# The head norm of the recurrent branch, moved into the merge stage of a two-model decoder kernel

## What is computed

```python
y_ret = retention(q, k, v, g, positions, ret_gn_g)
y_rwkv = rwkv7_time_mix(p_rwkv, ...)     # recurrent branch, 8 heads of 64
y_conv = short_conv(p_conv, conv_w)
gates = jax.nn.sigmoid((h @ w_gate + b_gate).astype(F32))
merged = jnp.zeros(x.shape, F32)
for i, y in enumerate((y_ret, y_rwkv, y_conv)):
    merged = merged + gates[..., i * d:(i + 1) * d] * (y @ w_branch[i])
x = x + (gate1[:, None, :] * (merged.astype(x.dtype) @ w_o)).astype(x.dtype)
```

```python
mu = jnp.mean(yf, axis=-1, keepdims=True)
var = jnp.mean(jnp.square(yf - mu), axis=-1, keepdims=True)
y = (yf - mu) * lax.rsqrt(var + eps) * g
y = y + jnp.sum(r * kt * r_k.astype(F32), axis=-1, keepdims=True) * v
return (y.reshape(bsz, seq, mw) * g).astype(p.dtype)
```

## Time and profile before

| | |
|---|---|
| median of 3 runs | 2585.14 us (2583.62 to 2586.28) |
| the profiled execution: time | 2586.32 us |
| the profiled execution: span from first to last instruction | 2584.5 us |
| its mean granted TensorE clock | 0.909 |
| recurrent head norm, first layer | 1064.47 to 1075.16 us |
| merge, first layer | 1075.45 to 1202.94 us |
| recurrent head norm, second layer | 1938.12 to 1948.65 us |
| merge, second layer | 1948.95 to 2076.66 us |

### The profile page before, as it was taken

How to read it: one execution, slowest core, us unless ns; L and a number is a source line. 1 busy time by engine, 2 the same in 40 slices (tenths; PEclk the granted TensorE clock), 3 DMA queues, 4 the chain that set the end, 5 groups by cost and what they waited for, 6 DMA issues and landing times. The chain is left out here.

```text
span 2584.5 us, 33377 instructions
## 1 busy us (share of the span) xinstructions
PE 2083.0 (81%) x14160; PEld 1300.0 (50%) x14161; DVE 634.1 (25%) x1404; ACT 359.0 (14%) x725; POOL 76.8 (3%) x104
## 2 busy tenths in 40 slices
PE   7888778889777999899867666689989988666665
PEld 5564336564333688788522222238887873222222
DVE  4451003551002235454200000022441121000001
ACT  1520001520002021200100000011211020000000
POOL 0201000201000000000000000000000000000000
PEclk9999989999988999999897888899999989888887
DMA  9358999255999332286899999973312369999996
GB/s 385 132 230 363 429 429 401 116 228 218 429 428 399 114 130 99 112 340 273 340 428 428 428 428 428 429 302 130 131 36 98 131 246 395 428 429 428 429 429 286
DMA packets 55841, 779.34 MB, mean 302 GB/s; under 512 B 6840, under 2 KB 7096, under 8 KB 8120
## 3 DMA queue, kind: packets, MB, share of 16 engines
q1 hardware_dynamic: 55736, 777.82, 72.5%
HBM read 776.75 MB, written 1.05 MB: 301 GB/s over the span
## 5 line engine op out<-in xcount | busy, mean ns | idle before, releaser
L1925 PE MATMUL bank<-ring,xnT 128*32 128x512 f32 x3136 | 488.6, 761 | 307.5 <-DMA ring<-in_w_exp 303.7
L1925 PEld LDWEIGHTS bank<-ring,xnT 128*32 128x32 f32 x3136 | 102.0, 125 | 683.7 <-DMA ring<-in_w_exp 450.3
L1950 PE MATMUL bank<-ring,arena 128*32 128x512 f32 x1440 | 178.6, 635 | 65.2 <-DMA ring<-in_w_exp 45.3
L965 PE MATMUL bank<-xnT,ring 128*128 128x256 f32 x960 | 210.7, 379 | 0.0
L2113 DVE TENSOR_TENSOR arena<-bank,arena 128x256 f32<-128x256 f32 (+1 forms) x33 | 18.3, 554 | 748.3 <-PE bank L1925 528.1
L965 PEld LDWEIGHTS bank<-xnT,ring 128*128 128x128 f32 x960 | 181.6, 190 | 28.4 <-issue 4.5
L1631 PE MATMUL bank<-xnT,ring 128*128 128x256 f32 x768 | 176.9, 384 | 10.1 <-PEq L843 10.1
L1631 PEld LDWEIGHTS bank<-xnT,ring 128*128 128x128 f32 x768 | 148.1, 193 | 32.3 <-issue 11.7
L1888 PE MATMUL bank<-arena,xnT 128*128 128x256 f32 x592 | 145.0, 400 | 3.6 <-DVE xnT L2124 3.6
L1888 PEld LDWEIGHTS bank<-arena,xnT 128*128 128x128 f32 x592 | 115.0, 200 | 64.3 <-issue 49.0
L1880 PE MATMUL bank<-arena 128*128 128x128 f32 x1056 | 133.3, 288 | 3.4 <-DVE arena L2033 3.4
(11 more groups left out here) (425 smaller groups left out, 2046.1 us busy)
## 6 DMA issues: line engine op xcount, KB each, us to landing
ring<-in_w_exp SPq DMA_DIRECT2D x274, 2048.0 KB, 25.6
arena<-in_w_ada SPq DMA_DIRECT2D x24, 2048.0 KB, 12.1
ring<-in_w_in SPq DMA_DIRECT2D x20, 2048.0 KB, 26.0
ring<-in_w_merge SPq DMA_DIRECT2D x18, 2048.0 KB, 8.0
arena<-in_w_exp SPq DMA_DIRECT2D x14, 2048.0 KB, 14.2
ring<-in_w_o SPq DMA_DIRECT2D x8, 2048.0 KB, 10.4
ring<-in_w_conv SPq DMA_DIRECT2D x6, 2048.0 KB, 7.9
ring<-in_w_rest SPq DMA_DIRECT2D x2, 1696.0 KB, 25.8
```

Source lines behind the costliest of these rows:

```text
L965: last = nc.tensor.matmul(o[:, T * j:T * j + T], w[:, k, col:col + P], xnT[:, k, :], start=k == 0, stop=k == KT - 1)
L1925: last = nc.tensor.matmul(o[rows(e), :], Xw[:, k, rows(e)], w[:, at:at + MW], start=k == 0, stop=k == KT - 1)
L1950: last = nc.tensor.matmul(o[rows(e), :], hidT[:, j, rows(e)], w[:, at:at + MW], start=j == 0, stop=j == ft - 1)
```

## The change

The block `head_norm` is gone. Its instructions now stand inside `merge`, which takes the branches in the order retention, convolution, recurrent. The weight chunks, the gate bias and the list `ys` follow that order.

```diff
+        BRANCHES = (0, 2, 1)
...
-                load(sp, n, dram["w_merge2"][l, n - MERGE])
+                load(sp, n, dram["w_merge2"][l, 3 * BRANCHES[(n - MERGE) // 3] + (n - MERGE) % 3])
...
+            mean_made, flat, sq_ready, var_made, log_ready, rstd_ready, normed = (sem(f"nwkv_{x}") for x in ("mean", "flat", "sq", "var", "log", "rstd", "done"))
+            ys = [(y_ret, y_rwkv, y_conv)[b] for b in BRANCHES]
+            y, nsq, gain = y_rwkv, ar(13824, MT, T), V2("rwkv_gn_g_2")
...
-            sg = ar(13824, 4, T)
+            sg = ar(16896, 4, T)
...
                 @block.sync
                 def _(sp):
                     if ahead:
+                        sp.wait_ge(normed, 1)
                         sp.dma_start(c_raw, dram["c_row"]).then_inc(c_in, 16)
...
                 @block.tensor
                 def _(pe):
+                    for i in range(2):
+                        nc.tensor.matmul(bank[4 + i][:, :], K("blk64"), y[:, 2 * i:2 * i + 2, :], start=True, stop=True).then_inc(mean_made, 1)
                     for i in range(3):
                         n = MERGE + 3 * i
                         for d in range(KT):
                             m = KT * i + d
+                            if m == 1:
+                                for a in range(2):
+                                    pe.wait_ge(sq_ready, a + 1)
+                                    nc.tensor.matmul(bank[6 + a][:, :], K("blk64"), nsq[:, 2 * a:2 * a + 2, :], start=True, stop=True).then_inc(var_made, 1)
+                            if m in (4, 5):
+                                pe.wait_ge(flat, m - 3)
+                            if m in (6, 7):
+                                pe.wait_ge(log_ready, m - 5)
+                            if m == 2 * KT:
+                                pe.wait_ge(normed, 1)
...
                 @block.scalar
                 def _(act):
+                    nc.scalar.preload_act_table_set("natural_log_exp_and_others")
+                    for i in range(2):
+                        act.wait_ge(flat, i + 1)
+                        nc.scalar.activation(nsq[:, 2 * i:2 * i + 2, :], y[:, 2 * i:2 * i + 2, :], ACT.Square).then_inc(sq_ready, 1)
+                    for i in range(2):
+                        act.wait_ge(var_made, i + 1)
+                        nc.scalar.activation(nsq[:, 2 * i:2 * i + 2, :], pair_of(bank[6 + i]), ACT.Ln, scale=1.0 / HD, bias=REPS).then_inc(log_ready, 1)
+                        act.wait_ge(log_ready, i + 1)
+                        nc.scalar.activation(nsq[:, 2 * i:2 * i + 2, :], nsq[:, 2 * i:2 * i + 2, :], ACT.Exp, scale=-0.5).then_inc(rstd_ready, 1)
...
                 @block.vector
                 def _(dve):
                     then = step(dve, s_dve)
+                    for i in range(2):
+                        dve.wait_ge(mean_made, i + 1)
+                        nc.vector.scalar_tensor_tensor(y[:, 2 * i:2 * i + 2, :], pair_of(bank[4 + i]), -1.0 / HD, y[:, 2 * i:2 * i + 2, :], ALU.mult, ALU.add).then_inc(flat, 1)
+                    for j in range(MT):
+                        dve.wait_ge(rstd_ready, j // 2 + 1)
+                        last = nc.vector.scalar_tensor_tensor(y[:, j, :], y[:, j, :], gain[:, j:j + 1], nsq[:, j, :], ALU.mult, ALU.mult)
+                    then(last)
+                    then(nc.vector.tensor_tensor(y, y, bonus, ALU.add))
+                    nc.vector.tensor_tensor(y, y, gT, ALU.mult).then_inc(normed, 1)
...
-                head_norm("nwkv", y_rwkv, ar(13824, MT, T), "blk64", HD, REPS, V2("rwkv_gn_g_2"), rwkv_finish)
                 merge(l)
```

More of the change, by code:

```diff
@@ L834, in load2 @@
                 load(sp, n, dram["w_exp2"][l, n - MOE2])
[L839 to L875, removed]
@@ L1599, in merge, with pair_of @@
             pair_ready, gate_ready, taken, s_dve = sem("mrg_pair"), sem("mrg_gate"), sem("mrg_taken"), sem("mrg_dve")
-            ys = (y_ret, y_rwkv, y_conv)
+            mean_made, flat, sq_ready, var_made, log_ready, rstd_ready, normed = (sem(f"nwkv_{x}") for x in ("mean", "flat", "sq", "var", "log", "rstd", "done"))
+            ys = [(y_ret, y_rwkv, y_conv)[b] for b in BRANCHES]
+            y, nsq, gain = y_rwkv, ar(13824, MT, T), V2("rwkv_gn_g_2")
+            def pair_of(b):
+                return b[:, :].rearrange("p (a t) -> p a t", a=2)
             ada, c_in, c_ready = ada_sems(), sem("mrg_c"), sem("mrg_cready")
@@ L1654, in _ @@
                                 act.wait_ge(taken, m - 3)
-                            nc.scalar.activation(sg[:, m % 4, :], bank[m % 8][:, 0:T], ACT.Sigmoid, bias=V2("b_gate_2")[:, m:m + 1]).then_inc(gate_ready, 1)
+                            nc.scalar.activation(sg[:, m % 4, :], bank[m % 8][:, 0:T], ACT.Sigmoid, bias=V2("b_gate_2")[:, KT * BRANCHES[i] + d:KT * BRANCHES[i] + d + 1]).then_inc(gate_ready, 1)
                 @block.vector
@@ L1713, in _ @@
                     norm_rstd(dve, norms)
-        def rwkv_finish(then):
-            then(nc.vector.tensor_tensor(y_rwkv, y_rwkv, bonus, ALU.add))
-            nc.vector.tensor_tensor(y_rwkv, y_rwkv, gT, ALU.mult)
         WIN = 32
```

## The result

The changed kernel takes 2568.35 us (median of 13 runs, 2562.72 to 2575.35) against 2585.14 us for the one before (13 runs, 2575.58 to 2592.68). The ratio is 0.994 with an interval of 0.9928 to 0.9952: 15.5 us less, 12.4 to 18.6. The ratio is formed from all runs; the two medians by themselves differ by 16.8 us. The forecast was 2570.4 us in a range of 2566.8 to 2574.8, a gain of 14.7. A stretch repeats to 0.1 or 0.2 us where the clock falls at the same place.

A forecast was written before the change was run, and what follows sets the result against it. The norm was taken as bound by engines passing data in turn, TensorE idling 5.03 us before the merge. Gains of 7.36 + 7.37 = 14.7 us off 2585.14 gave 2570.4 us, range 2566.8 to 2574.8.

The forecast's parts named there:

- The stretch: First mean matmul to tile 1's first matmul: from 17.75 us per layer to 10.39 and 10.38, gaining 14.7 in all.
- The means: Start of the stretch: left slow, 3.18 and 3.02 us to the next matmul; at full clock a layer needs 8.64.
- The clock at tile 0: Tile 0's gate matmuls: no second clock fall without the idle time; 3.75 and 3.90 us, against 5.04 before in the first layer.
- rival A: In or near tile 0 the clock falls once more although TensorE stays busy: gain 12.1 us, 2573.0 us; chance 0.13.
- TensorE's waits: In the merge, none expected from squares at m = 1 (slack 3.9 us), reused banks, or the finished norm at m = 16.
- `c_row` 4.7 us later: First layer, SP queue: `c_row` waits for the finished norm, issued some 15.6 us after the first mean matmul instead of 10.94.
- Level again by tile 8 or so: First merge: VectorE, 12 us behind TensorE, makes up 2 us a tile, needing 3.2 at most against 5.18.
- 19 us of slack: First merge, tile 8: first bank free at 1091.7, TensorE asks for it at 1111.2.
- the sign that the prediction named: In the merge's last tiles VectorE's waits are for ScalarE, not for `w_ada`.
- rival B: VectorE or `w_ada` keeps the first layer's lateness to the end of the merge: 2582.4 us; chance 0.03.
- D: SP queue: tile 16's ring load lands late; over 0.2% slower only if 62 us later, say 2592 us; chance 0.02.
- Rival C: Expert stages: the expert stream swallows the gain, some load already being bound by the stream: 2585.1 us; chance 0.03.

The follow-up runs named there:

- second profile: The changed kernel unchanged, run again as companion of later runs: 2565.89 us, ratio 0.9927 to the kernel before.
- experiment 1: Changed kernel with the branches in their old order (retention, recurrent, convolution), TensorE waiting for the finished norm at tile 8: 2569.66 us, ratio 0.995.
- experiment 2: Kernel before with only the new order of branches, the norm still in its own block: 2579.68 us, ratio 0.9991.
- experiment 4: Changed kernel with the variances ahead of tile 0 instead of behind it: 2570.01 us, ratio 0.9955.
- experiment 5: Changed kernel with N useless VectorE products before the norm's last one, N = 16, norm 20.2 us later: ratio 0.9986 to the kernel before.
- experiment 8: Changed kernel with 16 useless VectorE products, first merge's modulation products on half their columns: tile 1 to `project_out2` 128.0 us, first merge, single run.
- Experiment 3: Kernel before with five useless TensorE matmuls behind the norm's variances, filling the idle time ahead of the merge: 2577.87 us, ratio 0.9987.

## Why the prediction was right, step by step

**The stretch.** Predicted 10.39 and 10.38 us, measured 10.38 and 8.68, and 10.39 and 10.38 in the second profile. Piece by piece in the first layer: means to gates 3.15 us (3.18 expected), gates 3.79 (3.75), branch 1.73 (1.73), variances 1.71 (1.73). Experiments 1, 2 and 4 show that it is this stretch, and not the order of the branches or the swapped loads, that makes the gain.

**The means.** I left them slow in both layers. The clock fell under them in some executions only; where it did not, the stretch was 8.7 us, the bound that I had set at 8.64. In the second layer of the profile this mis-sized two terms, by 1.7 us in all: the means took 1.79 us to the gates instead of 3.02, and the gates 3.45 instead of 3.90.

**The clock at tile 0.** Over all eight profiles with the norm in the merge and tile 0 ahead of the variances, experiments included, there are 16 such stretches: five of 8.7 us (the clock never fell), nine of 10.25 to 10.39 (it was low under the means, as I had it), and two, in the second layer of experiments 5 and 8, of 11.24 and 11.43, where it had been low since the last matmuls of the recurrence and stayed so some way into tile 0. Their mean is 9.95 us, a gain of 7.8 us a layer or 15.6 in all, close to the 15.5 of the ratio. A fall that began at tile 0, rival A, is in none of them. The prediction took it that the slow starts follow idle time; the kernel before also had a fall with none (the last section), a row that spoke for A and that the prediction does not use. Experiment 3 shows 1.4 us a layer for the clock alone against 1.3 in the sum.

**TensorE's waits.** At m = 1, 4 to 7, 8 and 16 none, as forecast.

**ScalarE, VectorE and SP.** `c_row` 4.7 us later was right (15.59 us after the first mean matmul, 15.6 forecast). "Level again by tile 8 or so" and "19 us of slack" were wrong. VectorE waits for `w_ada` eight times, 27.2 us, and first waits for ScalarE again only at 1161.40, in tile 16. The step that failed counted VectorE's work per tile and the wait for tile 0's bank, and took the loads by their total of bytes and as paced by the ring, that is by TensorE. What SP waited for in the first merge shows the loop instead: 241 issues `w_ada` and waits for VectorE, 205 issues a ring load and waits for TensorE. Before, after, and with N = 16:

```profile
SPq L205 <- PE bank L1631: 63.6, 6, 17.9
...
SPq L241 <- DVE arena L250: 50.3, 7, 12.6
```

```profile
SPq L241 <- DVE arena L250: 62.0, 9, 13.5
...
SPq L205 <- PE bank L1613: 40.1, 5, 16.7
```

```profile
SPq L241 <- DVE arena L250: 84.6, 10, 13.9
...
SPq L205 <- PE bank L1613: 0.3, 1, 0.3
```

The later the norm, the less TensorE paces the queue and the more VectorE does. The loop must be level before the merge ends, and its real slack is 5 to 7 us beyond what the change uses. It did not matter for the result, as in the last tiles VectorE waited for ScalarE, the sign that the prediction named. But rival B was nearer than a chance of 0.03, and a slower kernel, which D put 62 us of lateness away by another path, is there with 40 us.

**The way to the end.** The gain passed through: tile 1 to `project_out2` kept its length, and the expert stages are no longer than before. Rival C fell. The measured 15.5 us and the forecast 14.7 agree within the interval.

**Slips and luck.** Rival A's upper end should be 2573.0 + 1.1 = 2574.1 us and not 2574.5, which added the spread downwards, and the last 0.3 us of the range's top have no term; nothing hangs on either. The starting point of 2585.14 us came from three runs, and the median of 13 is the same number; with runs that spread over 17 us that is luck. So is part of the near match of the totals: with the clock falling under the means in both layers the sum holds to 0.1 us (10.39 and 10.38 us in the second profile), but whether it falls differs from one execution to the next, and the prediction did not know that.

## What to carry to other kernels

A short stage in which three engines hand the same data round costs its whole length (11 us here). Laid beside independent output tiles it cost TensorE only its own matmuls, and 7.8 us a layer were gained on the mean of the profiles; the old order of branches would have done. Price an idle gap with the slow clock that may follow it. When work is delayed in a stage that also feeds another stream, measure the slack of that stream's loop (place free, load, use), not only the first buffer that will be missed.

## What had not been expected of the hardware

The clock's falls come and go between executions of one kernel at the same place: under the means of the second layer of the changed kernel (8.68 against 10.38 us for the stretch). They also come and go at the start of `project_out2`, after the same 2.0 us of idle time: 35.5 us for the stage in both layers of the kernel before and of experiment 1, 33.8 in both of the changed one, and one of each in experiment 2. In the second layer of the kernel before, the clock was at half already in the last matmuls of the recurrence, with TensorE busy all the time on tiles of 64 x 64:

```profile
1932.00:1935.00 3.00, 3.00 (x62) 3.00 (x60) 1.31 (x3) 0.00 (x0) 0.00 (x0) 0.50 0.02 5
```

It was at 1.00 again from 1936 to 1938 and fell a second time under the means, after 1.11 us of idle time. Such a fall cost 1.4 to 1.7 us where it came under the means, at tile 0 or in `project_out2`, and 2.8 us at tile 0 in the second layer of experiment 2, whatever the change under study did.
